# GpSimd and VectorE share the one-hots of the second key; the first five rows of u are gathered from the middle of the stage

## The reference, cut to what matters

```python
expert = idx1 * PEER_KEYS + idx2
gate = jax.nn.softmax(c_top, axis=-1)
...
u = u_table[eb]
hid = jax.nn.gelu(jnp.einsum('td,thkd->thk', xb, u), approximate=False) * gb
return jnp.einsum('thk,thkd->td', hid, v_table[eb])
```

## Time and profile before

| what | us |
|---|---|
| median of 3 runs | 3613.68 |
| the profiled execution, its own time | 3616.06 |
| its span, first to last instruction | 3614.3 |
| build stage, first hot_a to last product | 1549.2 to 1699.4 |
| main loop, from the first L1945 | 1707.2 on |

### The profile page before, as it was taken

How to read it: one execution, slowest core, us unless ns; L and a number is a source line. 1 busy time by engine, 2 the same in 40 slices (tenths; PEclk the granted TensorE clock), 3 DMA queues, 4 the chain that set the end, 5 groups by cost and what they waited for, 6 DMA issues and landing times.

```text
span 3614.3 us, 39996 instructions
## 1 busy us (share of the span) xinstructions
PE 3446.2 (95%) x11593; PEld 1976.7 (55%) x11593; DVE 2816.2 (78%) x6484; ACT 1078.7 (30%) x2721; POOL 1424.3 (39%) x1233
## 2 busy tenths in 40 slices
PE   7999989999997999768899999999999999999998
PEld 4666667777774566556444444444444444444443
DVE  2466686777774489899788888987888888888898
ACT  3233344444442222277221112111211122121212
POOL 1000000000001277400566565655565566655665
PEclk9999999999997999889999999999999999999999
DMA  3111012000002234247999999999999999999998
GB/s 112 30 36 35 0 50 91 23 23 29 29 35 114 50 70 80 34 136 208 396 392 375 394 382 393 378 379 355 395 373 382 389 399 376 375 394 377 388 377 328
DMA packets 313936, 829.65 MB, mean 230 GB/s; under 512 B 41504, under 2 KB 145056, under 8 KB 305056
## 3 DMA queue, kind: packets, MB, share of 16 engines
q0 software_dynamic: 165888, 537.01, 40.1%
q1 hardware_dynamic: 125104, 227.45, 17.4%
q10 hardware_dynamic: 22768, 63.18, 4.5%
HBM read 789.73 MB, written 37.81 MB: 229 GB/s over the span
## 4 chain that ended last, share of the span: by engine, by line
PE 49%; issue 4%; DVE 2%; DMA 1%; POOL 0%; ACT 0%; ACTq 0%; DVEq 0%; POOLq 0%
PE peer_ps_o L1958 24%; PE peer_ps_d L1945 22%; PE peer_ps_q L1886 2%; DMA peer_vr<-in_v_rows,peer_index 1%; DVE peer_mt L2133 0%; DVE peer_mt L2137 0%; DMA peer_ur<-in_u_rows,peer_index 0%; PE peer_ps_s L1896 0%; DVE Y L2173 0%; POOL peer_ur L1854 0%; POOL peer_vr L1861 0%; DVE peer_ur L2162 0%; PE peer_ps_o L1926 0%; DVE route_hit L1221 0%; DVE peer_chosen L1223 0%
## 5 line engine op out<-in xcount | busy, mean ns | idle before, releaser
L1854 POOL DMA_INDIRECT peer_ur<-in_u_rows,peer_index x512 | 568.9, 1111 | 608.9 <-DVE peer_ur L2162 401.6
L2173 DVE SCALAR_TENSOR_TENSOR Y<-peer_vr,osq,Y 128x1024 f32<-128x1024 f32 x512 | 657.0, 1283 | 90.4 <-DMA peer_vr<-in_v_rows,peer_index 88.2
L1861 POOL DMA_INDIRECT peer_vr<-in_v_rows,peer_index x512 | 585.7, 1144 | 321.6 <-issue 152.4
L2162 DVE SCALAR_TENSOR_TENSOR peer_ur<-peer_ur,Y 128x1024 f32<-128x1024 f32 x512 | 628.0, 1227 | 7.8 <-DMA peer_ur<-in_u_rows,peer_index 7.5
L1945 PE MATMUL peer_ps_d<-hnT,route_ut 128*128 128x512 f32 x1376 | 598.5, 592 | 0.0
L1958 PE MATMUL peer_ps_o<-hw,Y 128*128 128x512 f32 x1024 | 448.3, 598 | 12.8 <-DVE Y L2149 12.8
L1958 PE MATMUL peer_ps_o<-hnT,Y 128*128 128x512 f32 x1024 | 442.6, 592 | 0.0
L1945 PEld LDWEIGHTS peer_ps_d<-hnT,route_ut 128*128 128x128 f32 x1376 | 261.3, 190 | 327.7 <-issue 327.7
L1958 PEld LDWEIGHTS peer_ps_o<-hw,Y 128*128 128x128 f32 x1024 | 196.2, 192 | 255.8 <-issue 239.1
L1958 PEld LDWEIGHTS peer_ps_o<-hnT,Y 128*128 128x128 f32 x1024 | 193.5, 190 | 238.2 <-issue 238.2
L1945 PE MATMUL peer_ps_d<-hnT,peer_ut 128*128 128x512 f32 x672 | 295.2, 592 | 0.0
(11 more groups left out here) (331 smaller groups left out, 4945.9 us busy)
## 6 DMA issues: line engine op xcount, KB each, us to landing
route_ut<-in_u_cols SPq DMA_DIRECT2D x86, 512.0 KB
hw<-in_v_cols SPq DMA_DIRECT2D x16, 2048.0 KB
peer_mt<-sel ACTq DMA_DIRECT2D x64, 512.0 KB
hnT<-in_v_cols SPq DMA_DIRECT2D x16, 2048.0 KB
peer_ut<-in_u_cols SPq DMA_DIRECT2D x42, 512.0 KB
route_wk<-in_w_route ACTq DMA_DIRECT2D x14, 1024.0 KB
hnT<-in_w_route SPq DMA_DIRECT2D x9, 1024.0 KB
route_wk<-in_w_route SPq DMA_DIRECT2D x9, 1024.0 KB
```

The source lines that it names most:

```text
L1854: pool.indirect_dma_start(ur[:, r % RING, :], None, u_rows, bass.IndirectOffsetOnAxis(ap=index[:, r // TOPK % 4, r % TOPK:r % TOPK + 1], a ...
L1861: pool.indirect_dma_start(vr[:, r % RING, :], None, v_rows, bass.IndirectOffsetOnAxis(ap=index[:, r // TOPK % 4, r % TOPK:r % TOPK + 1], a ...
L2162: nc.vector.scalar_tensor_tensor(out=ur[:, s, :], in0=ur[:, s, :], scalar=1.0, in1=Y[:, b, D:MIX], op0=ALU.mult, op1=ALU.mult, accum_out=d ...
L2173: nc.vector.scalar_tensor_tensor(out=hb, in0=vr[:, s, :], scalar=hid[:, c:c + 1], in1=hb, op0=ALU.mult, op1=ALU.add).then_inc(comb_done, 1)
```

## The change

GpSimd gets the one-hots hot_b of tokens 2 and 3 of each group (`hot_rest`, two instructions of the form that VectorE uses), VectorE keeps tokens 0 and 1 (DVE_HOT = 2), and ScalarE makes none. TensorE waits for GpSimd in place of ScalarE. The fourth part of `pickedT` and its copy go. The first five gathers of u are issued by GpSimd behind its part of group 30 (U_ROWS_AT), no longer as soon as their indices are there.

```diff
--- before.py
+++ after.py
@@ -1699,7 +1699,7 @@
         mt = sb("mt", [P, 2, SEQ])
         chosen = sb("chosen", [P, TOPK])
         first_key = sb("first_key", [P, MB * P], U32)
-        pickedT = sb("pickedT", [P, 2, 4, P])
+        pickedT = sb("pickedT", [P, 2, 3, P])
         index = sb("index", [P, 4, TOPK], U32)
         gate = sb("gate", [P, 4, TOPK])
         fss, frs, dots, act_out, hid = osq[:, 0, :], osq[:, 1, :], osq[:, DB, :], osq[:, DB + 1, :], osq[:, DB + 2, :]
@@ -1745,7 +1745,7 @@
         fw_in = sem("fw_in")
         split_done, pick_turned, pick_out = sem("split_done"), sem("pick_turned"), sem("pick_out")
         hot_a_ready, hot_b_ready, sel_made, staged = sem("hot_a_ready"), sem("hot_b_ready"), sem("sel_made"), sem("staged")
-        last_apart, last_ready = sem("last_apart"), sem("last_ready")
+        hot_rest_ready = sem("hot_rest_ready")
         sel_out = [sem(f"sel_out{i}") for i in range(4)]
         x_turned, x_out = sem("x_turned"), sem("x_out")
         u_in, m_in, v_in = ([sem(f"u_in{i}") for i in range(UT)], [sem(f"m_in{i}") for i in range(2)],
@@ -1765,6 +1765,8 @@
         HALVES = 2 * MB * P // SELB
         LATE_PICKS = {40: 2}
         ROUTE_AT = (24,)
+        DVE_HOT = 2
+        U_ROWS_AT = 30
         END = PAIRS
 
         def sel_stores(i):
@@ -1848,6 +1850,16 @@
 
         @block.gpsimd
         def _(pool):
+            def hot_rest(j):
+                b, t = j // (P // 4), j % (P // 4) * 4
+                pool.wait_ge(pick_out, b + 1)
+                need(pool, sel_made, j - 1)
+                for q in range(DVE_HOT, 4):
+                    ins = nc.gpsimd.tensor_scalar(hot_b[j % 2][:, q, :], R.count[:],
+                                                  pickedT[:, b % 2, 1, t + q:t + q + 1],
+                                                  pickedT[:, b % 2, 2, t + q:t + q + 1], ALU.is_equal, ALU.mult)
+                ins.then_inc(hot_rest_ready, 1)
+
             def u_row(r):
                 pool.wait_ge(R.routed, DU + r // TOPK + 1)
                 need(pool, dot_done, r - RING + 1)
@@ -1862,8 +1874,11 @@
                                         bass.IndirectOffsetOnAxis(ap=index[:, r // TOPK % 4, r % TOPK:r % TOPK + 1], axis=0)
                                         ).then_inc(got_v[r % RING], 16)
 
-            for r in range(RING):
-                u_row(r)
+            for j in range(M_GROUPS):
+                hot_rest(j)
+                if j == U_ROWS_AT:
+                    for r in range(RING):
+                        u_row(r)
             pool.wait_ge(sel_out[3], sel_stores(3))
             for r in range(RING):
                 v_row(r)
@@ -1920,7 +1935,7 @@
                     turn_picks(LATE_PICKS[j])
                 pe.wait_ge(hot_a_ready, j + 1)
                 pe.wait_ge(hot_b_ready, j + 1)
-                pe.wait_ge(last_ready, j + 1)
+                pe.wait_ge(hot_rest_ready, j + 1)
                 need(pe, staged, 2 * (j - 1))
                 for q in range(4):
                     mm = nc.tensor.matmul(ps_o[:, j % 2, q * P:(q + 1) * P], hot_a[j % 2][:, q, :], hot_b[j % 2][:, q, :],
@@ -1983,19 +1998,7 @@
             def pick_copy(b):
                 act.wait_ge(pick_turned, b + 1)
                 need(act, sel_made, (b - 1) * (P // 4))
-                nc.scalar.activation(pickedT[:, b % 2, 0:3], ps_t[:, 0:3, :], ACT.Copy)
-                nc.scalar.activation(pickedT[:, b % 2, 3], ps_t[:, 2, :], ACT.Copy, scale=-1.0).then_inc(pick_out, 1)
-
-            def hot_last(j):
-                b, t = j // (P // 4), j % (P // 4) * 4 + 3
-                act.wait_ge(pick_out, b + 1)
-                need(act, sel_made, j - 1)
-                to = hot_b[j % 2][:, 3, :]
-                nc.scalar.activation(to, R.count[:], ACT.Abs, scale=-1.0,
-                                     bias=pickedT[:, b % 2, 1, t:t + 1]).then_inc(last_apart, 1)
-                act.wait_ge(last_apart, j + 1)
-                nc.scalar.activation(to, to, ACT.Relu, scale=pickedT[:, b % 2, 3, t:t + 1],
-                                     bias=pickedT[:, b % 2, 2, t:t + 1]).then_inc(last_ready, 1)
+                nc.scalar.activation(pickedT[:, b % 2], ps_t[:, 0:3, :], ACT.Copy).then_inc(pick_out, 1)
 
             def place_out(j, hh):
                 x = j // PER_BATCH * 2 + hh
@@ -2062,14 +2065,10 @@
 
             pick_copy(0)
             pick_copy(1)
-            hot_last(0)
-            hot_last(1)
             for j in range(M_GROUPS):
                 if j in LATE_PICKS:
                     pick_copy(LATE_PICKS[j])
                 place_out(j, 0)
-                if j + 2 < M_GROUPS:
-                    hot_last(j + 2)
                 place_out(j, 1)
                 if j in ROUTE_AT:
                     gates(DU + ROUTE_AT.index(j))
@@ -2133,7 +2132,7 @@
                 nc.vector.tensor_tensor(hot_a[j % 2], R.count[:].unsqueeze(1).to_broadcast([P, 4, KEYS]),
                                         pickedT[:, b % 2, 0, t:t + 4].unsqueeze(2).to_broadcast([P, 4, KEYS]),
                                         ALU.is_equal).then_inc(hot_a_ready, 1)
-                for q in range(3):
+                for q in range(DVE_HOT):
                     ins = nc.vector.tensor_scalar(hot_b[j % 2][:, q, :], R.count[:], pickedT[:, b % 2, 1, t + q:t + q + 1],
                                                   pickedT[:, b % 2, 2, t + q:t + q + 1], ALU.is_equal, ALU.mult)
                 ins.then_inc(hot_b_ready, 1)
```

## The result

The changed kernel takes 3665.3 us (median of 4 runs, 3664.2 to 3668.0), the one before 3613.9 beside it: a ratio of 1.0143, 95% interval 1.0126 to 1.0161, 51 us slower. Slower was forecast, by 20 us; the 51 lie inside the range (3604 to 3685), 31 us beyond the forecast. The profiled execution of the kernel after took 3664.2 us, its span is 3662.1.

What follows compares the result with a forecast made beforehand. The build stage's two-group VectorE-TensorE loop, 1.40 us a group, was taken as the bound, with VectorE and ScalarE within 0.03. Exclusion +14.4, gathers +4.7 and clock +1 made +20 us: 3634 us against 3613.7, range 3604 to 3685.

Steps and rivals of the forecast that it cites:

- The loop and what VectorE's relief is worth: Build stage: two-group loop VectorE-TensorE-VectorE, 2.80 us or 1.40 a group; without one hot_b 1.27, gaining 12.2 us before the gathers' stall.
- ScalarE's relief alone: Build stage: two instructions a group leave ScalarE, 0.83 of its 1.43 us; claimed worth 0, as VectorE's loop stays at 1.40.
- I take 0.35 ... I put the upper end at 0.50: Build stage: length in us of one GpSimd one-hot, 128 columns, judged from a select and a two-tensor product.
- Alone that fits: Build stage: GpSimd's two instructions, 0.70 us a group, fit without interference; its loop of 2.35 is under VectorE's 2.55.
- GpSimd's own: Build stage: the loop through GpSimd and TensorE, 0.70 plus 1.35 plus perhaps 0.3 for its wait, 2.35 us.
- The exclusion: Build stage: VectorE and GpSimd exclude each other; 0.55 us a group on VectorE's loop, 1.55 against 1.40, +14.4 us.
- rows 10: Profile rows before the change: a GpSimd instruction issued at 510.43 takes 1.54 not 1.04 us, ending 0.90 after VectorE's L780.
- The period: Build stage: time per group, forecast 1.55 us against 1.40 before; the forecast case spans 1.42 to 1.7, chance 0.40.
- in full series: Build-stage rival: nothing overlaps, 1.81 us a group, 3659 us; with 0.50 us instructions 2.11, 3688 us; chance 0.26.
- signs of being wrong: Profile after: VectorE's durations unchanged (about 3606 us), GpSimd's instruction over 0.5 us (3690 and more), or opening swallows the shift.
- The gathers and the clock: Build stage, group 31: five gathers of u ahead of hot_b stall it, +4.7 us; lower TensorE clock after the pause, +1.
- The opening and the main loop: Behind the build stage: a later build moves the opening one for one; the main loop keeps its length, shifted.

## Why the prediction was right or wrong

*The loop and what VectorE's relief is worth: right.* 1.27 us a group and -7.5 us in all with GpSimd at no cost; the run without its one-hots gave 1.27 and -8.6. That ScalarE's relief alone gains nothing rests on the loop and isn't shown: no run took ScalarE's share away by itself.

*"I take 0.35 ... I put the upper end at 0.50": the step that failed, and with it "Alone that fits".* GpSimd's one-hot takes 0.79 us, 0.77 from start to start, twice my figure and outside my bounds. I made the bounds from a select and a product of two tensors, 0.92 and 1.67 ns a column; this form costs 3.3. With 2 x 0.77 = 1.54 us even GpSimd's own queue is longer than VectorE's 1.27 a group. What binds is the loop that I had called "GpSimd's own" and set at 0.70 + 0.3 for its wait + 1.35 for TensorE = 2.35 us, under VectorE's 2.55. It measured 3.71: 1.53 for the two instructions, 0.69 for the wait, the whole of hot_a, and 1.49 for TensorE. The Trainium skill, page "GPSIMD Engine Reference", section "4.1 Engine selection", has one-input work on GpSimd at roughly line rate; at 3.3 ns a column, against 1.67 for two inputs here, this trace doesn't agree, and a bound drawn from other forms doesn't hold for a compare with a product.

*The exclusion: right that it costs, wrong in direction and place.* I laid 0.55 us a group on VectorE's loop. What was measured is 0.31 us (0.18 and 0.43 in turn, 28 us in all), and on GpSimd, whose pair started 0.22 or 0.48 us behind hot_a in turn and waited for its end both times. VectorE's instructions were hardly held: hot_b took at most 0.345 us, and seven of the 96 hot_a took over 0.70, the longest 0.84, where none did before. The Trainium skill, page "SBUF — State Buffer", section "Who interferes with whom", which I cited, lets whoever issues first keep the pair for a whole instruction. For hot_a that held: GpSimd waited for its end. For GpSimd it didn't: hot_a, begun at 1713.11 while the instruction of 1712.56 still ran, took its usual 0.69 us, VectorE's hot_b ran in 0.34 beside a TENSOR_SCALAR of GpSimd, and hot_a was held by one seldom, by 0.15 us at the most in this kernel, though GpSimd's two-tensor product had held VectorE for 0.41. The stretch of rows 10, GpSimd held by VectorE, was the row that carried over.

*The period.* 1.55 forecast, 1.86 measured, 3.71 / 2. In the steady rows that is +0.46 a group where I had 0.15. Over the whole stage, with the gathers moved to its end, it came to 38.7 us where I had 14.4; the groups before took somewhat more than 1.40 us outside the steady rows. Length and exclusion work together: with instructions of 0.35 us the same loop would be 0.69 + 0.70 + 1.49 = 2.88 us, 1.44 a group, an estimate from the rows above that no run shows; without the exclusion it took 1.54 to 1.57, as the run without VectorE's one-hots shows. 1.86 is near the 1.81 of my rival "in full series", to which I gave 0.26, but not by its mechanism: there VectorE's 1.11 and GpSimd's 0.70 went in turn; here hot_a, GpSimd's pair and TensorE go in turn, and VectorE idles a third of the time. That the time fell into my range is luck in this sense: the upper end came from that rival. Two of my signs of being wrong came, VectorE's durations unchanged and GpSimd's instruction over 0.5 us, and with neither the time that I had put beside it (3606, and 3690 or more).

*The gathers and the clock: too small.* +4.7 and +1 forecast; with the gathers at the end the stage was 11.2 us shorter: 6.4 us by the pause, 2.6 in the nine groups behind it, at the lower clock, and 2.0 by something that I hadn't seen, the last one-hot held by two dot products, an exclusion like the others.

*The opening and the main loop: right.* They moved with the stage: 49.9 us in the stage, 47.8 in the span, 51.3 in the medians. The first gather of v came 18.6 us behind the start of the last product, 18.8 before.

## What to carry to other kernels

Before work goes to GpSimd, price its instruction in just that form and size, in a short run if no row has it; an instruction of another kind on the same engine was off by two here. Then lay out the loop that goes through the new engine, with what VectorE does at the same moment: here hot_a starts when TensorE is done and ends behind the start of GpSimd's pair, in nearly every group, so the whole of hot_a stands ahead of the pair and is paid each time. An engine that shows as full can be one that is held: ask what a shorter instruction would give back, half of it here. GpSimd's help paid only as one instruction a group, with a third buffer and with all three engines near the same length.

## What the runs showed of the hardware

A TENSOR_SCALAR with compare and product and two numbers per partition took GpSimd 0.79 us for 128 x 128 and 0.57 for 128 x 64; without the product and its number 0.60, with constants 0.64. VectorE does it in 0.34. Against VectorE's instruction with two inputs in SBUF it waited to the end each time (up to 1.38 us in place of 0.79, 2.63 beside two dot products), against VectorE's TENSOR_SCALAR of 128 x 128 it waited little (0.84 on average). It held VectorE's TENSOR_SCALAR by 0.07 us in most groups with one instruction of GpSimd a group (0.41 in place of 0.34) and not at all in the kernel after, and hot_a rarely, by up to 0.15 us there (0.84 in place of 0.69).
